# Final sum of a mixture-of-experts layer: the read-back of four of nine token tiles moves from the sync engine's DMA queue to ScalarE's

## What is computed

```
x = x + merged @ w_out
x = x + hier_moe(rmsnorm(x, g_ffn), ...)     # two experts for each row, weights w2
y_prompt = rmsnorm(xp, g_final)
y_sample = rmsnorm(xs, g_final)
```

## Time and profile before

| | us |
|---|---|
| median of 3 runs | 944.74 (944.39 to 945.12) |
| time of the profiled execution | 945.64 |
| its span | 943.8 |
| around the span | 1.84 |

### The profile page before, as it was taken

The page is one execution under the profiler, slowest core; times in us unless marked ns, Lnnn a source line. Parts: engine busy times, 40 slices in busy tenths (PEclk is TensorE's granted clock), DMA queues, the critical chain, the costliest instruction groups (busy, mean ns, idle before and its releaser), DMA issues.

```text
span 943.8 us, 13479 instructions
## 1 busy us (share of the span) xinstructions
PE 919.0 (97%) x5016; PEld 814.3 (86%) x5016; DVE 698.5 (74%) x951; ACT 441.7 (47%) x694; POOL 83.3 (9%) x109
## 2 busy tenths in 40 slices
PE   8999999999999999999999999999999999999984
PEld 7999999999999999999888888778787878787741
DVE  5648797777888877537722348899898989999847
ACT  6612221312112138923301334687878787878714
POOL 0000000010000000000000002322121212121100
PEclk9999999999999999999999999999999999999998
DMA  9020111111111211012511766599999999999559
GB/s 302 12 68 23 45 46 45 40 37 45 56 34 46 90 45 45 23 34 81 183 45 37 277 228 245 180 368 391 376 386 376 373 362 357 380 377 381 198 200 373
DMA packets 73801, 170.13 MB, mean 180 GB/s; under 512 B 10907, under 2 KB 48299, under 8 KB 60401
## 3 DMA queue, kind: packets, MB, share of 16 engines
q1 hardware_dynamic: 64529, 152.05, 44.9%
q0 software_dynamic: 9216, 17.32, 5.7%
HBM read 156.83 MB, written 22.47 MB: 190 GB/s over the span
## 4 chain that ended last, share of the span: by engine, by line
PE 88%; DVE 5%; ACT 4%; issue 1%; DMA 1%; SPq 0%; ACTq 0%; DVEq 0%
PE ps L1675 40%; PE ps L1956 16%; PE ps L1863 11%; PE ps L1934 10%; PE ps L1949 3%; PE ps L1912 2%; PE ps L1817 2%; PE ps L1698 1%; DVE x L1649 1%; PE ps L1985 1%; PE ps L1804 1%; ACT C L884 1%; DVE x L1635 1%; PE ps L1920 1%; DVE hT L1084 1%
## 5 line engine op out<-in xcount | busy, mean ns | idle before, releaser
L1675 PE MATMUL ps<-hT,w_hi 128*128 128x352 f32 x1344 | 328.6, 326 | 1.5 <-DVE hT L1084 0.8
L1675 PEld LDWEIGHTS ps<-hT,w_hi 128*128 128x128 f32 x1344 | 235.0, 188 | 2.9 <-DVE hT L1084 1.2
L1675 PE MATMUL ps<-hT,w_lo 128*128 128x352 f32 x672 | 218.0, 324 | 0.0
L1158 DVE SCALAR_TENSOR_TENSOR C<-V,w_dw,C 128x1086 f32<-128x1086 f32 x120 | 154.8, 1343 | 0.3
L1524 DVE TENSOR_TENSOR wgu_lo<-wgu,wgu_hi 128x1024 fp32r<-128x1024 f32 (+1 forms) x128 | 133.7, 1086 | 1.3 <-ACT wgu_hi L989 1.1
L1675 PEld LDWEIGHTS ps<-hT,w_lo 128*128 128x128 f32 x672 | 125.9, 187 | 0.0
L989 ACT ACTIVATE wgu_hi<-wgu 128x1024 fp32r<-128x1024 f32 x124 | 114.9, 956 | 6.5 <-PE ps L1956 5.3
L1956 PE MATMUL ps<-wgu_hi,XT_hi 128*128 128x512 f32 x224 | 100.0, 447 | 0.0
L1551 DVE TENSOR_TENSOR wdn_lo<-wdn,wdn_hi 128x1024 fp32r<-128x1024 f32 x62 | 73.2, 1223 | 27.3 <-ACT wdn_hi L1025 27.3
L1091 DVE TENSOR_TENSOR w_lo<-w_raw,w_hi 128x1024 fp32r<-128x1024 f32 (+1 forms) x44 | 45.2, 1027 | 62.7 <-ACT w_hi L791 62.7
L1863 PE MATMUL ps<-wo_hi,hT 128*128 128x512 f32 x288 | 91.6, 399 | 0.0
(11 more groups left out here) (258 smaller groups left out, 1490.0 us busy)
## 6 DMA issues: line engine op xcount, KB each, us to landing
wgu<-in_w_gate SPq DMA_DIRECT2D x32, 1024.0 KB, 7.9
wgu<-in_w_up SPq DMA_DIRECT2D x32, 1024.0 KB, 9.9
wdn<-in_w_down SPq DMA_DIRECT2D x32, 1024.0 KB, 10.7
w_raw<-in_w_in SPq DMA_DIRECT2D x28, 512.0 KB, 3.8
yy<-YK SPq DMA_DIRECT2D x8, 1024.0 KB, 12.1
xs<-in_x_prompt SPq DMA_DIRECT2D x8, 512.0 KB, 7.5
wo_raw<-in_w_out SPq DMA_DIRECT2D x8, 512.0 KB, 4.9
xr<-in_x_prompt SPq DMA_DIRECT2D x16, 256.0 KB, 2.7
```

Of the source, the lines that this page charges most:

```text
L1158: op = dve.scalar_tensor_tensor(out=C[:, g, :], in0=V[:, g, k:k + CWID], scalar=w_dw[:, g, k:k + 1], in1=C[:, g, :], op0=ALU.mult, op1=ALU ...
L1675: op = pe.matmul(ps[:, bank_of(m, c), 0:CH], a[s][:, k, :], r[:, k, c * CH:(c + 1) * CH], start=(k == 0 and q == 0), stop=(k == K - 1 and ...
```

## The change

Of the nine loads of `yy`, SP keeps those of tiles 8, 0, 2, 4, 6. Those of tiles 1, 3, 5, 7 (`ADDED[1:]`) are issued by ACT, on ACT's own DMA queue, after its small root and ahead of its squares. ACT first waits for `s_yy[8]`, that is until the load of tile 8, which SP issues first, has landed. Source, destination, size and semaphore of each load are as before, and so are all waits for them.

```
             for t in TAIL:
                 n = P if t < TILES - 1 else LAST
-                sp.dma_start(yy[0:n, t], YK.rearrange("(t k) d -> t k d", k=2)[t * P:t * P + n]).then_inc(s_yy[t], 16)
+                if t not in ADDED[1:]:
+                    sp.dma_start(yy[0:n, t], YK.rearrange("(t k) d -> t k d", k=2)[t * P:t * P + n]).then_inc(s_yy[t], 16)
             for i, t in enumerate(TAIL):
                 store(i, t)
...
             act.activation(sumsq[:, 0:1], eps_rms[:], ACT.Sqrt).then_inc(s_yend, 1)
+            act.wait_ge(s_yy[TILES - 1], 16)
+            for t in ADDED[1:]:
+                act.dma_start(yy[:, t], YK.rearrange("(t k) d -> t k d", k=2)[t * P:(t + 1) * P]).then_inc(s_yy[t], 16)
             for i, t in enumerate(TAIL):
                 n = P if t < TILES - 1 else LAST
                 if t in SUMMED:
```

## The result

The changed kernel takes 948.62 us (median of 16 runs, 948.0 to 951.26) against 945.3 us for the kernel before in 16 runs beside it. The ratio is 1.0035, with a 95% interval of 1.0029 to 1.0042, so it is 3.3 us slower (2.7 to 4.0). The profiled execution took 948.23 us with a span of 946.2 us.

The account below looks back on a forecast made before the run. The prediction took PE's chain to bound the tail until 920.30, then ACT to 921.80, then DVE. Its parts summed 0 + 0 + 1.2 us onto 944.74, giving 945.9 us; likeliest case 945.4 to 946.6, 8-in-10 range 944.2 to 948.0.

Parts of the forecast that it names:

- DVE's chain from add(3) on has no slack: DVE's tail after 921.80: no idle time, so whatever starts an instruction late moves the end by as much.
- SP's four issues fewer: SP's load issues in the tail: 1.7 us of SP's time saved, gain nothing.
- ACT's four issues: ACT between its root and tile 8's square: done at 913.9 within idle time, cost nothing.
- half of the engines each: Tail loads on two queues: equal shares, so a pair of tiles takes 4.9 us; called the unproved step.
- The last store: End of the kernel: the last store still lands 2.6 us after its issue.
- part 3: Order in which the tail's loads flow: each odd tile falls one place behind its even neighbour, costing 1.2 us.
- 1.2 us late: DVE's add(3): tile 3 lands at 924.35 to 924.4 against a start at 923.20.
- DVE's slack up to 921.80: DVE before tile 0's reciprocal: idle 1.56 us waiting for ACT; a later add(1) leaves 0.2 us of it.
- Smaller share, 948.6: Tail loads: ACT's queue gets a third of the engines, tile 3 lands about 927.1, 3.9 us late; chance 0.17.
- tile 3 after 925.1: Landing of tile 3's load: later than this, 1.9 us late, decides for ACT's queue getting the smaller share.
- Hidden anyway: Tail loads: ACT's queue gets ahead and odd tiles land before they are needed, 944.4 to 945.2 us; chance 0.20.
- Faster: Whole kernel: two queues move the loads more quickly and DVE's chain profits, 942.5 us or less; chance 0.04.

Follow-up runs that it names:

- The order alone: Kernel before with all nine loads on SP in the order 8, 0, 2, 1, 4, 3, 6, 5, 7: 1.0018, 1.7 us slower (0.9 to 2.6).
- third profile: The kernel before, unchanged, profiled again, without PE's low clock or slow loads up to add(3): 945.36 us, tail 27.7 us.
- the run with tile 1 alone: Against the kernel before, only tile 1's load goes to ACT's queue and SP issues the other eight: 1.0020, 1.9 us slower (1.0 to 2.7).
- a version that cared for DVE's alone: The changed kernel, but SP waits until tile 0 has landed before issuing tiles 2, 4, 6: 1.0044 against the kernel before, 4.2 us slower (2.8 to 5.5).
- the run with the roles swapped: Against the kernel before, ACT issues tiles 2, 4, 6 after tile 8's landing, SP issues 8, 0, 1, 3, 5, 7: 1.0005, 0.5 us.

## Why the prediction was wrong

The time was 3.3 us up where 1.2 us was forecast, beyond the range.

**Right.** DVE's chain from add(3) on has no slack, so a late tile moves the end by as much. SP's four issues fewer gave nothing. ACT's four issues took 1.79 us (911.53 to 913.32) and were done 0.9 us before its first square at 914.23. Once both ran, the two queues had half of the engines each: 5.0 us from tile 1 to tile 3 and from tile 2 to tile 4. The last store was unaffected. The order alone, as a one-queue experiment, moved add(3) by 1.0 us, which the forecast put at 1.2.

**The step that failed** is in part 3: "tiles 2 and 1 are both in by the time at which tile 2 was in before, 919.4". I let ACT's half begin as soon as tile 0 had flowed. Counted from add(8), tile 1 should have come after 7.3 us and tile 3 after 12.2; they came after 9.1 and 14.0, both 1.8 us later. The windows of the queues show the step itself: tile 1 was issued at 911.53 and its first packet moved at 915.0, 3.5 us later. SP's own first load, on idle engines, was issued at 908.24 and its first packet moved about 1 us later, at 909.0. Until 915.0 SP's tile 2, issued earlier, went on alone, and it landed 3.4 us after tile 0 instead of 4.9. The term "1.2 us late" for add(3) measured 2.9 us.

**A second flaw, in the scale.** The forecast read DVE's slack up to 921.80 from one profile, and PE's low clock had made that slack (5.40 us for eight matmuls instead of 3.70). Against the third profile of the kernel before, the tail of the change is 3.9 us longer and not 2.9. The order alone was forecast at 1.2 us and measured 1.7 (0.9 to 2.6), so the size of this flaw is not clear of the noise.

**What the runs show in its place.** The lateness is two parts: the order that half shares give (1.0 us in the tail, 1.7 us measured with one queue), and the late start of the queue that comes second, the other 1.6 us or so. The second part is not a first use of the queue, and not a property of ACT's: SP's tile 2 took the same 9.0 us when it was the second. It goes with what the first queue has lined up. With tiles 2, 4, 6 behind tile 0, ACT's tile 1 took 9.1 us and its first packet 3.5 us; without them 4.7 us, and its first packets moved 1.1 to 1.4 us after the issue, as tile 0's ended.

**The rivals.** "Smaller share, 948.6" names the time that was measured, and the sign set for it, tile 3 after 925.1, came up: counted from add(8), tile 3 came at 926.1 on the scale of the earlier trace rows. That is luck, since its mechanism did not happen. SP's tiles 2, 4, 6 would all have been in 13.4 us after add(8); tile 6 came after 15.9, and the shares were equal. "Hidden anyway" needed tile 3 by 923.2. Faster did not occur. By the forecast the late tile 1 pushed finish(0) by 0.2 us; it pushed it by 1.9 us, from 9.66 to 11.57 us after add(8), and the run with tile 1 alone was 1.9 us slower.

**The Trainium skill** (DMA: Bandwidth & Descriptors, Issuing engines are not separate DMA queues) says that loads started by different engines run on the same 16 DMA engines and interleave. The trace agrees: the throughput stayed at 428 GB/s. By its rule that a second issuing engine only saves issue time, no difference was to be expected, and the forecast gave that 0.20; 3.3 us more were measured, and the measurement decides.

**Open.** The traces show when the second queue's packets begin, and that it depends on what the first queue has lined up; why they wait is not shown. That the engines had already taken in packets of the first queue fits 4.7 against 9.1 us and tile 0's 9.9 us when it was second by 0.4 us, but how much they take in was not measured. All measured differences lie 0.2 to 1.9 us above the difference between the run's tail and that of the earlier trace rows; the 27.7 us tail of the third profile makes up to 1.0 us of that plausible, but this is not shown.

## What to carry to other kernels

In this kernel the DMA engines were full, and a second issuing engine moved no more bytes per us; it changed when each load landed. The loads issued late on it came late: 9 us for 1 MB instead of the 5 us between two tiles at half share. Before moving loads, write down for each when it lands and when its reader's turn comes, for every engine that reads, and put on the second queue those with the most time in between. Moving PE's tiles cost nothing that could be told, moving DVE's cost 3.3 us, and a version that cared for DVE's alone lost 4.2 us at PE's tile, part of it because PE, kept waiting, also lost its clock.

## What was not expected of the hardware

- Two queues shared evenly only once both were running. Of two loads issued 0.4 us apart, tile 1 landed 6.4 us and tile 0 9.9 us after its issue; with 0.5 us between tile 0 and tile 1 the other way round, tile 0 took 5.4 us and tile 1 9.2 us.
- PE's granted clock fell to 1.2 GHz for some 3 us after an idle stretch of 2.09 and 1.94 us in two profiles of the kernel before, and stayed at 2.4 GHz after 1.95 us in another, after 2.03 us in the run that starts ACT after tile 0's issue, and after 2.10 us in the run with the roles swapped. Where it fell ahead of the loads, the kernel's tail was 1 us longer than in the third profile.
- The pace of the loads in the unchanged kernel was 2.45 us a tile, up to tile 5, in three profiles and 2.7 us in one. The slack of 1.4 us that tile 3 has in the earlier trace rows was gone in that execution.
